# Two transformer blocks on one core: mixer steps set between weight pieces, output projections by input halves

## What is computed

```python
for l in range(DEPTH):                       # first block, 2 layers
    h = rms_norm(x, norm1_g[l]) * (1.0 + sc1) + sh1
    z, xbc, dt_raw, mq, mk, mv, sq, sk, sv = split(h @ w_in[l])
    y_ssd  = ssd_mixer(z, xbc, dt_raw, ...)  # conv, 8 decay matrices, norm of y * silu(z)
    y_moba = moba_attention(mq, mk, mv, ...) # 4 heads; at 256 tokens plain causal attention
    y_swa  = swa_attention(sq, sk, sv, ...)  # 4 heads, window 128
    x = x + g1 * (concat([y_ssd, y_moba, y_swa]) @ w_out[l])
    h = rms_norm(x, norm2_g[l]) * (1.0 + sc2) + sh2
    x = x + g2 * peer_ffn(h, ...)            # 16384 experts, top 16 of 8 heads
for l in range(DEPTH):                       # second block, 2 layers
    x = x + 0.5 * rms_norm_2(swiglu(rms_norm_2(x), ...))
    x = x + rms_norm_2(hybrid_mixer(rms_norm_2(x), ...))   # NSA and retention
    x = x + rms_norm_2(memory_xattn(rms_norm_2(x), rms_norm_2(mem), ...))
    x = x + 0.5 * rms_norm_2(swiglu(rms_norm_2(x), ...))
```

## Time and profile before

| | us |
|---|---|
| median of 3 runs | 3641.87 (3641.11 to 3643.89) |
| the profiled execution, its own time | 3642.42 |
| its span in the trace | 3640.6 |
| PE busy in the span | 3371.6 (93%) |
| mean granted TensorE clock, share of full | 0.956 |

### The profile page before, as it was taken

The page is one execution under the profiler, slowest core; times in us unless marked ns, Lnnn a source line. Parts: engine busy times, 40 slices in busy tenths (PEclk is TensorE's granted clock), DMA queues, the critical chain, the costliest instruction groups (busy, mean ns, idle before and its releaser), DMA issues.

```text
span 3640.6 us, 55813 instructions
## 1 busy us (share of the span) xinstructions
PE 3371.6 (93%) x22132; PEld 3074.8 (84%) x22132; DVE 2403.5 (66%) x4114; ACT 1475.0 (41%) x1559; POOL 229.4 (6%) x48
## 2 busy tenths in 40 slices
PE   6879999999998799999999989896989899968898
PEld 2879999888888789999998879785989797968897
DVE  6657997777886669985557765464545454645454
ACT  1434444343334434453333343452443434444433
POOL 0005700000000028100000000000000000000000
PEclk8989999999999899999999999997999999979999
DMA  9414467778884234566667755450435455423353
GB/s 367 180 60 162 162 221 250 273 270 282 283 285 159 79 139 174 196 241 211 214 213 238 245 220 186 166 213 16 174 141 184 170 181 179 174 82 137 139 180 138
DMA packets 165989, 690.04 MB, mean 190 GB/s; under 512 B 11701, under 2 KB 78029, under 8 KB 92249
## 3 DMA queue, kind: packets, MB, share of 16 engines
q1 hardware_dynamic: 161432, 663.84, 51.5%
q10 hardware_dynamic: 4290, 22.54, 1.7%
HBM read 650.66 MB, written 35.68 MB: 189 GB/s over the span
## 4 chain that ended last, share of the span: by engine, by line
PE 81%; DVE 11%; ACT 3%; issue 2%; DMA 1%; DVEq 1%; PEld 1%; ACTq 0%; PEldq 0%
PE ps L743 25%; PE ps L989 19%; PE ps L749 13%; PE ps L776 9%; PE ps L783 4%; PE ps L967 3%; ACT work L1218 1%; DMA work<-in_mem 1%; DVE position_hot L1929 1%; PE ps L715 1%; DVE position_hot L1932 1%; DVE scr L1894 1%; DVE scr L1887 1%; DVE work L1888 1%; PE ps L1040 1%
## 5 line engine op out<-in xcount | busy, mean ns | idle before, releaser
L1226 ACT ACTIVATE weights_upper<-weights 128x2048 fp32r<-128x2048 f32 x520 | 996.3, 1917 | 1699.9 <-PE ps L743 901.3
L1613 DVE TENSOR_TENSOR weights_lower<-weights,weights_upper 128x2048 fp32r<-128x2048 f32 x476 | 1096.2, 2304 | 727.9 <-ACT weights_upper L1226 726.8
L743 PE MATMUL ps<-hT_upper,weights_upper 128*128 128x256 f32 x4416 | 626.7, 284 | 3.0 <-ACT hT_upper L1444 3.0
L743 PE MATMUL ps<-hT_lower,weights_upper 128*128 128x256 f32 x4416 | 627.8, 285 | 0.2
L743 PEld LDWEIGHTS ps<-hT_lower,weights_upper 128*128 128x128 f32 x4416 | 573.3, 192 | 7.0 <-issue 3.5
L749 PE MATMUL ps<-hT_upper,weights_lower 128*128 128x256 f32 x4416 | 575.3, 283 | 4.1 <-POOL weights_lower L680 4.1
L743 PEld LDWEIGHTS ps<-hT_upper,weights_upper 128*128 128x128 f32 x4416 | 572.8, 193 | 6.3 <-ACT hT_upper L1444 5.9
L749 PEld LDWEIGHTS ps<-hT_upper,weights_lower 128*128 128x128 f32 x4416 | 549.7, 192 | 4.9 <-POOL weights_lower L680 4.9
L680 POOL TENSOR_TENSOR weights_lower<-weights,weights_upper 128x2048 fp32r<-128x2048 f32 x44 | 229.2, 5221 | 1238.1 <-ACT weights_upper L1226 1238.1
L989 PE MATMUL ps<-weights_upper,hidden_lower 128*128 128x512 f32 x1024 | 254.7, 391 | 0.0
L989 PE MATMUL ps<-weights_upper,hidden_upper 128*128 128x512 f32 x1024 | 252.9, 389 | 0.0
(11 more groups left out here) (319 smaller groups left out, 3502.8 us busy)
## 6 DMA issues: line engine op xcount, KB each, us to landing
weights<-in_parts SPq DMA_DIRECT2D x264, 1024.0 KB, 4.8
weights<-in_experts SPq DMA_DIRECT2D x256, 1024.0 KB, 4.9
scr<-gates SPq DMA_DIRECT2D x32, 1024.0 KB, 8.3
weights<-in_ada_w SPq DMA_DIRECT2D x12, 2048.0 KB, 12.9
work<-in_ada_s SPq DMA_DIRECT2D x96, 256.0 KB, 5.3
gates<-h SPq DMA_DIRECT2D x16, 1024.0 KB, 4.8
gates<-work SPq DMA_DIRECT2D x16, 1024.0 KB, 4.8
mod<-in_row ACTq DMA_DIRECT2D x3, 1536.0 KB, 6.3
```

The costliest lines, as they stand in the source:

```text
L743: m = mm(bank[:, e * T:(e + 1) * T], up[:, c, e * P:(e + 1) * P], s_[:, c, :], start=(e == 0 and n == 0 and c == 0), stop=False, skip_grou ...
L1226: f(upper[:, p_.r % SPLIT, :], raw[:, p_.r, :], ACT.Copy).then_inc(upper_ready, 1)
L1613: v.tensor_tensor(lower[:, s, :], raw[:, p_.r, :], upper[:, s, :].bitcast(F32), ALU.subtract)\
```

## The change

- **First mixer.** The input projection goes in the order xbc (4 pieces), wint (2), mq (2), sq (2), z (2), with `seg`, `mS`, `xs`, `cb`, `sS` set between them. All eight decay matrices have a place of their own (`Ldec`, 8 x 384), so that exp and product are made in place. DVE does small steps of dt between the taps; ACT instead of DVE takes q and k.
- **Output projections** `wout` and `nout`: pieces ordered by input halves, so that both column halves get the attention (or retention) inputs first and the scan (or NSA) inputs last; norm and transposes are made for each half apart.
- **Second mixer.** nin (6 pieces), wS, nsv (2), lS, ret (4), rS, rv (2), wPT, rO, cw1 (4), wO, hidT, lPT, kc, rg (1), cS, lO, cPT, rg (1), cO, then oT and nout. The 64 small `position` instructions on DVE become 10 larger ones.
- **Constants multiplied.** Ahead of five kinds of transposes, nine in all over the layers, PE multiplies the identity by 512 columns of constants (`keep_busy`) into the bank that the transposes will use: 7 times for hT of layer 1, 4 for each h2T, 8 for f1T, 6 for nT, 5 for f2T.

```diff
+            def keep_busy(k, name, n):
+                pe.wait_ge(*k.free(name, 0))
+                for _ in range(n):
+                    mm(k.bank(name, 0), ident, cst[:, 0:NBLK], start=True, stop=True, skip_group_check=True)
...
-                parts_by_token(k, 0, "win", 0, 0, src=hT1, fresh=(k, "hT", "upper1", l * 12))
-                for i in range(8):
-                    parts_by_feature(k, 0, "winf", i, src=hT1)
+                for i in range(4):
+                    parts_by_feature(k, 0, "xbc", i, src=hT1, fresh=(k, "hT", "upper1", l * 12))
                 parts_by_token(k, 0, "wint", 0, 0, cols=392, src=hT1)
...
-                transposes(k, "yT", h, "ycat", l * TT)
-                parts_by_token(k, 0, "wout", 0, 0, src=hT1, fresh=(k, "yT", "upper1", l * 12 + 4))
-                parts_by_token(k, 0, "wout", 2, 2, src=hT1)
-                transposes(k, "h2T", h, "h2", l * TT)
+                for i in range(4):
+                    if i % 2 == 0:
+                        signal, banks = ("att_out", (2, 3)) if i == 0 else ("ssd_out", (0, 1))
+                        transposes(k, "yT", h, signal, l * TT, banks=banks)
+                    half_by_token(k, 0, "wout", i, src=hT1, fresh=(k, "yT", "upper1", l * 12 + 4, True))
+                transposes(k, "h2T", h, "h2", l * TT, busy=4)
...
-                    scaled_transposes(k, f + "T", (l * 4 + n) * TT)
+                    scaled_transposes(k, f + "T", (l * 4 + n) * TT, busy=5 if n else 8)
...
# DVE, first mixer, after the taps and the dt steps between them:
+                seg_in(0)
+                seg_in(1)
+                ahead("mq", 0, 2)
+                seg_in(2)
+                seg_in(3)
+                ahead("sq", 0)
...
# DVE, second mixer:
+                ahead("rg", 0, 2)
+                v.drain()
+                for t in range(TT):
+                    v.wait_ge(*k.emptied("rg", t))
+                    v.tensor_tensor(h[:, t, 512:D], ro[:, t, :], gr[:, t, :], ALU.mult).then_inc(S("ret_out"), 1)
+                combine("cO", 0)
+                lower_tokens(k, "oT", hT2[1], "upper2", l * 8, (2, 3))
...
+                ahead("nout", 0)
+                lower_tokens(k, "oT", hT2[1], "upper2", l * 8 + 2, (0, 1))
+                ahead("nout", 1)
```

More of the change, by code:

```diff
@@ new lines, in _ @@
+                maxima("wS", near, 24, "wmax")
+                ahead("nsv", 0, 2)
+                maxima("lS", sel, 72, "lmax")
+                ahead("ret", 0, 4)
+                for i in range(RH):
+                    v.wait_ge(*k.filled("rS", i))
+                    v.tensor_tensor(rS[i], k.bank("rS", i)[:, 0:384], retm[:, i, :], ALU.mult)\
+                        .then_inc(k.empty_sem("rS", i), 1)
+                ahead("rv", 0, 2)
+                for t in range(TT):
+                    take(k, "rv", t, vr[:, t, :])
```

757 lines of the change are left out of this document (419 added, 338 removed).

## The result

| | before | after |
|---|---|---|
| median of 4 runs, us | 3642.88 (3641.11 to 3643.91) | 3559.11 (3558.34 to 3559.94) |
| the profiled execution, its own time | 3642.42 | 3559.32 |
| its span | 3640.6 | 3557.5 |
| mean granted TensorE clock | 0.956 | 0.979 |

The changed kernel takes 0.9771 of the time before, 95% interval [0.9754, 0.9787]: 83.8 us less, where 101 were forecast (3541). The direction was right, the time lies inside the range, and 17 to 18 us of the expected gain did not come. Where they stayed is the question of all that follows.

A forecast was written before the change was run, and what follows sets the result against it. PE's in-order program was taken as the bound, its mixer steps waiting for DVE or ACT. First mixers -35, second mixers -62 and constants -4 made -101 from 3642.4, 3541.4, with the median forecast at 3541 us; range 3516 to 3582.

The forecast's parts named there:

- Forecast -17.5 each: First mixer of each layer: 19.5 us fewer by the walk, less 2 given back for half clock; -35 over both.
- The walk along three engines: First mixer from the end of xbc 0: PE, DVE and ACT followed with row durations; 7.4 us of idle time left.
- banks under 1: First mixer, seg 4 and 5: they take xs's banks, which DVE empties at 170 to 171; under 1 us lost.
- the clock's term: Second mixer: waits at the end make half clock likely, so 3.3 us of the gain given back per iteration.
- 151 of work + 18.4 idle + 3.3 half clock: Second mixer window: full-clock work, remaining waits and clock allowance; predicted gain 31 us per iteration, 62 in all.
- Forecast -4: Constants ahead of transposes: -6 us together from avoided half clock, +2 in iteration 2.
- The +2 in iteration 2: f1T, iteration 2: constants wait for f2d's bank and end 3.9 us late, less 2 gained at full clock.
- Turns at half clock: Rival: transposes run at half clock wherever they stand, some 22 us in all, 3563 us; chance 0.12.
- Copies come late: Rival: a quarter of the 80 woven pieces lose 2 us each to late ACT/DVE parts, 3581 us; chance 0.16.
- Slower: Rival: PE waits 2.29 us for the lower part at each of 80 woven pieces, 3724 us; chance 0.04.
- The weave does more: Rival: fewer remaining waits than walked and no clock loss, 3520 us; chance 0.11.
- the signs that I named: Profile after: windows 118 to 121 and 169 to 173 us, waits at seg 0, oT, nout 2, late iteration-2 constants.

The follow-up runs named there:

- the maxima first: Changed kernel with DVE taking the maxima of the window scores ahead of rounding the position sums: 3555.6 us.
- the version with all edits together: Changed kernel with wide compressed scores, nout 2's upper part early, maxima before position sums, sq 0 before seg 0, wait-filling constants, reordered retention gate: 3504.6 us.

## Why the prediction was right, and where it was off

- **First mixers: right.** Forecast -17.5 each; measured -19.0 and -18.0. The walk along three engines found the waits where they are: 4.4 us at seg 0 (4.33), banks under 1, wout 0 1.6 (0.81 in two parts), wout 2 0.6 (0.56). Idle time is 6.2 us where 7.4 were written, half clock 1.5 where 2 were given back, work 111.2 where I had 111. (The steps on DVE as I listed them end at 149.2, not at 148.7; it changes nothing, as the dt steps were put at "some 4.5".)
- **Second mixers: mechanism right, the clock's term too small.** I wrote 151 of work + 18.4 idle + 3.3 half clock = 172.7; measured are, in iteration 1, 179.2 = 153.5 + 15.1 + 10.6. Idle time was over-estimated by 3.3 (oT waited 2.01, not 4.0; nout 0 waited 1.66 for 1.5, nout 2 4.50 for 5.7), the work under-estimated by 2.5, and the half clock by 7.3. The step that failed is the sentence "The waits at the end make half clock likely for a few us: I give back 3.3". It looked for half clock only behind waits at the end. 3 us came there. Between 1 and 2 came behind nsv's wait of 2.12 us, which I had in my list without a clock price (in iteration 1 alone; iteration 2 is 1.1 us shorter), and 6 to 7 behind cS, with no wait at all.
- **Why cS escaped.** I built the full-clock work by taking each stretch's half-clock share out, and cS was among those at half clock before. I took it for a victim of the wait ahead of it. That was so, as the run of the kernel before with wide scores shows; that it would also be a cause, once it ran at full clock, no row could show, and the run with wide scores does.
- **Constants: nothing where I had a gain.** Forecast -4; the run without them is 1.1 us faster. The +2 in iteration 2 was right, by the right mechanism, the bank of f2d's last result. The gains failed because I let a row of what full clock is worth stand for what the wait leaves of it: the constants end 3.2 to 4.6 us ahead of the transposes, and in my own a wait of 3.60 us was enough to lose the clock. I used that row for seg 0 and not here. And the sizes were too large besides: with the waits filled, the eight places gave 2.3 us and not 6.
- **The halves** carried no term of their own in the sum. They give 5 to 6 us a layer in the first block and nothing in the second.
- **Rivals.** *Turns at half clock* fell: in mid-mixer the 24 turns of lPT take 3.1 us, 0.128 each, and the 12 of mPT 1.47. The Trainium skill, "TensorE: Matmul & The Clock Gate", Part 4, PE-mode transpose, says that full clock does not engage for transposes; here it neither kept them slow nor fell during 24 of them in a row, so the trace disagrees. (With the maxima first it did fall as the turns of lPT began, once, and rose again while they ran.) *Copies come late* did not happen but for nout 2, which was in the walk. *Slower* did not either; the run with doubled lower parts shows that with 2.3 us more of DVE time a piece the gain is gone. *The weave does more* was reached only by the version with all edits together.
- **The bounds held.** The time lies inside 3516 to 3582, near the case of turns at half clock (3563) by coincidence: that case had the right amount of lost clock for another reason. Of the signs that I named, the lengths of the first mixers, the 4 us at seg 0, the waits at nout 2 and the late constants in iteration 2 came; the second mixers are 5 to 6 us longer than the upper end that I named, and oT waits 2.0 us, not 3 to 5.

## What to carry to other kernels

When idle time is removed from an engine with a gated clock, count what will then run at full clock for the first time, and ask of each such step whether it keeps the clock by itself: here products of 15 columns cost the same time as products of 128 and were followed by half clock. A wait of 2 to 4 us on PE can cost about its own length again in half clock (with doubled lower parts 17.2 us for 18.4), and at 2 us it did so in some iterations and not in others; so give every wait that a walk leaves a price in clock, as a range. A wait filled with constants helped only where it was filled to its end and from a bank that was free at its beginning. And when a woven order leaves waits, look first for an engine that stands idle with the needed copy standing behind another wait in its program.

## What the runs showed of the hardware

- Sixteen products of 15 columns (32 instructions in 3.98 us) take the same time as sixteen of 128 columns (4.17 us). The narrow ones ran at full clock at first, and the clock fell 2.4 to 5.0 us after their start, in both iterations of eight traces (the changed kernel and the seven edits of it that keep this row unbroken), and stayed at half for 13.7 or 17.1 us. With the wide ones it stayed at 1.00 until the wait at oT in both iterations of three traces. 8.5 to 11.3 us of the kernel hang on it.
- Narrow scores are not the only thing without a long wait that the clock falls behind: with the maxima first it fell once, in the turns of lPT, 11 us ahead of them.
- Changing between 64-row f32 products and 128-row products of rounded parts, one to one, costs 0.27 us a pair at full clock (0.75 for 0.48).
- The same wait can lose the clock or keep it. nsv's 2.12 us were followed by half clock in iteration 1 of the changed kernel and not in iteration 2; with more constants it was the other way round. At oT 2.0 us kept the clock in both iterations of the changed kernel, and 2.02 lost it in one with the maxima first. The 2.83 + 1.67 us of nout 2 were followed by 7 us at half in both.
- After constants, 0.67 + 1.67 us of waiting at h2T kept the clock through the transposes in three of four cases (two kernels, two layers), though in one of these it fell within 2 us behind them; 3.23 + 1.67 us lost it in both layers of the changed kernel.
